# An encoder's dilated attention: the undilated head group over nearby keys with a softmax of its own, and the attention steps staggered anew

## The reference

```python
B_GROUPS = ((128, 1), (512, 4), (2048, 16))      # (window, dilation), 4 heads each
def dilated_attention(q, k, v, window, dilation):
    # to_sub gathers each residue class mod dilation by stride
    o, lse = banded_attention(to_sub(q), to_sub(k), to_sub(v), (window // 2) // dilation, None)
...
    qa, ka, va = ...                              # 8 query heads, 2 key heads, |i-j| <= 128, with sinks
    ya, _ = banded_attention(qa, ka, va, A_HALF_WINDOW, a_sink[l])
    for gi, (win, dil) in enumerate(B_GROUPS):
        o, lse = dilated_attention(qg, kg, vg, win, dil)
        outs.append(o); lses.append(lse)
    wg = jax.nn.softmax(jnp.stack(lses, axis=0), axis=0)
    yb = jnp.sum(wg[..., None] * jnp.stack(outs, axis=0), axis=0)
    merged = jax.nn.sigmoid(parts[-2]) * ya + jax.nn.sigmoid(parts[-1]) * yb
    x = x + jnp.einsum('bsd,de->bse', merged, w_out[l])
```

## Time and profile before

| | before |
| --- | --- |
| time, median of 3 runs | 1340.33 us (1340.04 to 1347.6) |
| profiled execution, its own time | 1341.68 us |
| span of the profiled execution | 1339.9 us |
| mean granted TensorE clock | 0.972 |
| PE busy | 1216.8 us (91%) |
| PEld (weight load, beside PE) | 798.0 us (60%) |
| DVE busy | 574.7 us (43%) |
| ACT busy | 410.5 us (31%) |
| POOL busy | 232.7 us (17%) |

### The profile page before, as it was taken

One profiled execution on the slowest core, in us unless ns is written; L12 is line 12 of the kernel. 1 busy time (PEld: TensorE's weight loads), 2 busy tenths in 40 slices (PEclk: granted clock), 3 DMA queues, 4 the chain that ended last, 5 costly groups with the idle time before them and its releaser, 6 DMA issues.

```text
span 1339.9 us, 17202 instructions
## 1 busy us (share of the span) xinstructions
PE 1216.8 (91%) x6364; PEld 798.0 (60%) x6364; DVE 574.7 (43%) x1359; ACT 410.5 (31%) x768; POOL 232.7 (17%) x179
## 2 busy tenths in 40 slices
PE   6999989999999999888599999899999989988981
PEld 5777767888876343332177777678887844433320
DVE  5567676333345222221455777743333442222115
ACT  5334346333342110000334443563332411110002
POOL 0314140122201111111012323302221011111100
PEclk9999999999999999899899999999999889999996
DMA  5432221553556999999823323126537379999995
GB/s 213 119 99 88 79 80 33 173 203 107 208 219 208 420 426 422 424 421 411 306 81 95 97 92 95 33 79 209 168 96 297 141 278 411 423 424 424 420 412 221
DMA packets 69566, 306.62 MB, mean 229 GB/s; under 512 B 11968, under 2 KB 12224, under 8 KB 59248
## 3 DMA queue, kind: packets, MB, share of 16 engines
q1 hardware_dynamic: 58624, 282.45, 56.0%
q0 software_dynamic: 10720, 22.37, 4.5%
q10 hardware_dynamic: 144, 0.77, 0.2%
HBM read 290.34 MB, written 23.07 MB: 234 GB/s over the span
## 4 chain that ended last, share of the span: by engine, by line
PE 64%; DMA 12%; SPq 8%; DVE 8%; ACT 4%; issue 2%; DVEq 2%; POOLq 0%; ACTq 0%
PE bank L508 13%; PE bank L510 13%; PE bank L509 13%; PE bank L792 10%; DMA gu<-in_gu_w 9%; SPq L368 5%; PE bank L808 5%; SPq L373 3%; DMA raw<-in_stream 2%; PE bank L648 2%; PE bank L787 1%; DVE prob L1295 1%; PE bank L618 1%; DVEq L1272 1%; PE bank L588 1%
## 5 line engine op out<-in xcount | busy, mean ns | idle before, releaser
L792 PE MATMUL bank<-gu,xgt 128*64 128x512 f32 x1024 | 237.8, 613 | 39.8 <-DMA gu<-in_gu_w 38.0
L508 PE MATMUL bank<-h_hi,w_hi 128*128 128x512 f32 x640 | 253.3, 396 | 8.1 <-DVE w_lo L1175 4.0
L510 PE MATMUL bank<-h_hi,w_lo 128*128 128x512 f32 x640 | 249.5, 390 | 0.0
L509 PE MATMUL bank<-h_lo,w_hi 128*128 128x512 f32 x640 | 249.1, 389 | 0.0
L792 PEld LDWEIGHTS bank<-gu,xgt 128*64 128x64 f32 x1024 | 74.8, 141 | 198.8 <-issue 150.8
L1175 DVE TENSOR_TENSOR w_lo<-raw,w_hi 128x1024 fp32r<-128x1024 f32 x102 | 124.4, 1220 | 145.8 <-ACT w_hi L920 144.5
L508 PEld LDWEIGHTS bank<-h_hi,w_hi 128*128 128x128 f32 x640 | 120.1, 188 | 34.8 <-issue 8.1
L510 PEld LDWEIGHTS bank<-h_hi,w_lo 128*128 128x128 f32 x640 | 120.1, 188 | 25.7
L509 PEld LDWEIGHTS bank<-h_lo,w_hi 128*128 128x128 f32 x640 | 120.3, 188 | 23.6
L920 ACT ACTIVATE w_hi<-raw 128x1024 fp32r<-128x1024 f32 x102 | 107.5, 1054 | 59.7 <-PE bank L510 56.2
L808 PE MATMUL bank<-dn,zt 128*64 128x512 f32 x512 | 117.2, 599 | 6.3 <-ACT zt L1134 2.8
(11 more groups left out here) (173 smaller groups left out, 1600.5 us busy)
## 6 DMA issues: line engine op xcount, KB each, us to landing
gu<-in_gu_w SPq DMA_DIRECT2D x18, 4096.0 KB, 31.6
raw<-in_stream SPq DMA_DIRECT2D x112, 512.0 KB, 3.6
dn<-in_dn_w SPq DMA_DIRECT2D x18, 2048.0 KB, 32.3
gu<-in_gu_w SPq DMA_DIRECT2D x32, 1024.0 KB, 14.9
dn<-in_dn_w SPq DMA_DIRECT2D x20, 1024.0 KB, 19.0
gu<-in_gu_w SPq DMA_DIRECT2D x32, 512.0 KB, 4.9
swp<-pj SPq DMA_DIRECT2D x136, 64.0 KB, 2.2
dn<-in_dn_w SPq DMA_DIRECT2D x16, 512.0 KB, 5.5
```

The source lines that it names most:

```text
L508: mm(dst, ah, bh, start=start, stop=False)
L509: mm(dst, ah, bl, start=False, stop=False)
L510: return mm(dst, al, bh, start=False, stop=stop)
L792: last = mm(bank[b][e * CAP:(e + 1) * CAP, :], xgt[:, x_s, k, e * CAP:(e + 1) * CAP], gu[w_s][:, e, k, :], start=k == 0, stop=k == KD - 1)
```

## The change

The undilated group keeps its queries and keys in natural order. A step's 128 queries then need 256 keys only, in two runs of 128 (`CHUNKS`), and the near and the two far groups get softmaxes of their own: `max_b` and `sum_b` hold minimum and sum of each, the near values go to bank 7 and the far ones to bank 3, and at the end the near weight is the sigmoid of the difference of the log-sums (`logs`, `lse`, `mix`, `near_weight`, `join`), which PE spreads over 64 rows by matmuls of a repeated column with the identity. Values come one step late in all steps, scores three ahead; the 16 tiles are spread over steps 0 to 11, 13, 14, 16 and 18 (`FILLED`); ACT copies the transposed probabilities before it does the exponentials. In the last block of tiles the values tiles come after queries and keys.

```diff
+BLOCK_C = BLOCK_B[3:] + BLOCK_B[:3]
+BLOCKS = [BLOCK_A, BLOCK_B, BLOCK_C]
...
+FILLED = (*range(12), 13, 14, 16, 18)
+NB = 2 * NSTEP_B
+CHUNKS = [(0, 1), (1, 2), (2, 3), (3, 0)]
+def score_bank(u, h):
+    if u < NSTEP_A:
+        return (2, 0, 1, 3)[2 * (u % 2) + h]
+    return (2 * (u - NSTEP_A) + h + 2) % 3
...
-    order += [("scores", 0), ("scores", 1)]
+    order += [("scores", 0), ("scores", 1), ("scores", 2)]
...
-    for u in range(NSTEP_A):
+    for u in range(STEPS):
         order.append(("transpose", u))
-        next_tile()
-        order.append(("scores", u + 2))
-        order.append(("values", u))
-    next_tile()
-    order.append(("scores", NSTEP_A + 2))
-    for u in range(NSTEP_A, STEPS):
-        order.append(("transpose", u))
-        if u > NSTEP_A:
+        if u in FILLED:
+            next_tile()
+        elif waiting:
+            order.append(("turn", waiting.pop(0)))
+        if u == STEPS - 5:
+            order.append(("split", NQ))
+        if u == STEPS - 4:
+            order.append(("split", NQ + 1))
+        if u == STEPS - 3:
+            order += [("gate", 0), ("lse", 0)]
+        if u == STEPS - 2:
+            order.append(("split", NQ + 2))
+        if u:
             order.append(("values", u - 1))
         if u + 3 < STEPS:
             order.append(("scores", u + 3))
-        if u == STEPS - 4:
-            order.append(("split", NQ))
-        if u == STEPS - 3:
-            order.append(("gate", 0))
-    order += [("values", STEPS - 1), ("gate", 1)]
+    order += [("mix", 0), ("mix", 1), ("join", 0), ("values", STEPS - 1), ("join", 1), ("gate", 1)]
...
-                        pe.wait_ge(ptd_ok, l * NSTEP_A + len(before))
+                        pe.wait_ge(pta_ok, l * STEPS + len(before))
+                        pe.wait_ge(ptd_ok, l * NSTEP_A + min(len(before), NSTEP_A))
...
+                        if u > NSTEP_A:
+                            pe.wait_ge(mh_ok, l * NB + u - NSTEP_A)
+                        c0, c1 = CHUNKS[r]
+                        for n in ([None] if c0 and c1 else [0, 1]):
+                            for h in range(2):
+                                rows = slice(h * DH, (h + 1) * DH)
+                                dst = bank[score_bank(u, h)]
+                                if n is None:
+                                    mm(dst[:, 0:MG], qk[rows, 0, cols], qk[rows, 1, c0 * P - 64:(c1 + 1) * P - 64], start=True, stop=True)
+                                else:
+                                    mm(dst[:, n * P:(n + 1) * P], qk[rows, 0, cols], chunk(qk[rows, 1, :], CHUNKS[r][n]), start=True, stop=True)
...
+                        parts_of = [(7, [(vb[:, 0, k, :], n * P) for n, k in enumerate(CHUNKS[t])]),
+                                    (3, [(vb[:, g, t, :], (g + 1) * P) for g in (1, 2)])]
+                    for b, terms in parts_of:
+                        for n, (v, c0) in enumerate(terms):
+                            for h in range(2):
+                                last = mm(bank[b][h * DH:(h + 1) * DH, cols], v[:, h * DH:(h + 1) * DH], pt[u % 2][:, h, c0:c0 + P],
+                                          start=n == 0, stop=n == len(terms) - 1)
...
+                def mix(p, l=l):
+                    if p == 0:
+                        pe.wait_ge(lse_ok, l + 1)
+                        pe.wait_ge(pj_act, (l + 1) * NQ)
+                        need(pe, mx_ok, (l + 1) * STEPS)
+                    dst = bank[6 if p == 0 else 2]
+                    for kind in range(2):
+                        for t in range(TT):
+                            for h in range(2):
+                                one = 4 * (p * NSTEP_B + t) + 2 * h + kind
+                                half = dst[h * DH:(h + 1) * DH, :]
+                                out = by_residue(half)[:, t, :, :] if kind else half[:, t * P:(t + 1) * P]
+                                last = mm(out, lse_b[:, one:one + 1].to_broadcast([P, DH]), ident, start=kind == 0 and t == 0,
+                                          stop=kind == 1 and t == TT - 1)
+                    last.then_inc(dm_ok, 1)
...
+                            for kind in range(2):
+                                p = prob[u % 3][:, h, kind * MG:(kind + 1) * MG]
+                                one = 4 * (u - NSTEP_A) + 2 * h + kind
+                                last = run(p, p, ACT.Exp, bias=max_b[:, one:one + 1], scale=-1.0, accum_out=sum_b[:, one:one + 1])
...
+                    last = run(pt[u % 2][:, 0, 0:width(u)], bank[4][:, 0:width(u)], ACT.Copy)
+                    if u >= NSTEP_A:
+                        last = run(pt[u % 2][:, 1, :], bank[5][:, :], ACT.Copy)
+                    last.then_inc(pta_ok, 1)
...
+                def logs(l=l):
+                    act.wait_ge(ex_ok, (l + 1) * STEPS)
+                    run(lse_b, sum_b, ACT.Ln).then_inc(ln_ok, 1)
+                    run(spare, ms[:, 0:1], ACT.Sigmoid)
+                def near_weight(p, l=l):
+                    act.wait_ge(dm_ok, l * 2 + p + 1)
+                    run(w_near[:, p, :], bank[6 if p == 0 else 2][:, :], ACT.Sigmoid).then_inc(wn_ok, 1)
+                def join(p, l=l):
+                    act.wait_ge(of_ok, l * 2 + p + 1)
+                    run(o_hi[:, 4 + p, :], o_near[:, p, :], ACT.Copy).then_inc(ohi_ok, 1)
...
+                        if i + 2 < STEPS:
+                            exps(i + 2)
...
+                    if u >= 3:
+                        dve.wait_ge(tr_ok, l * STEPS + u - 2)
...
+                            v.tensor_tensor_reduce(out=prob[u % 3][:, h, 0:MG], in0=src[:, 0:MG], in1=mask_b[:, (r + 1) // 2, :],
+                                                   scale=-SCALE, scalar=3.0e38, op0=ALU.add, op1=ALU.min, accum_out=max_b[:, one:one + 1])
+                            last = v.tensor_tensor_reduce(out=prob[u % 3][:, h, MG:MB], in0=src[:, MG:MB], in1=mask_b12[:, :],
+                                                          scale=-SCALE, scalar=3.0e38, op0=ALU.add, op1=ALU.min,
+                                                          accum_out=max_b[:, one + 1:one + 2])
+                            last.then_inc(mx_ok if h else mh_ok, 1)
...
+                def lse(l=l):
+                    dve.wait_ge(ln_ok, l + 1)
+                    logs, tops = (a.rearrange("p (n k) -> p n k", k=2) for a in (lse_b, max_b))
+                    tt(logs[:, :, 0], logs[:, :, 0], tops[:, :, 0], ALU.subtract)
+                    tt(logs[:, :, 1], tops[:, :, 1], logs[:, :, 1], ALU.subtract).then_inc(lse_ok, 1)
+                def join(p, l=l):
+                    dve.wait_ge(wn_ok, l * 2 + p + 1)
+                    o = o_near[:, p, :]
+                    v.drain()
+                    tt(o, o, w_near[:, p, :], ALU.mult)
+                    v.drain()
+                    tt(o, o, o_far[:, p, :], ALU.add).then_inc(of_ok, 1)
+                    dve.wait_ge(ohi_ok, l * 6 + 4 + p + 1)
+                    tt(o_lo[:, 4 + p, :], o, o_hi[:, 4 + p, :].bitcast(FP32), ALU.subtract).then_inc(olo_ok, 1)
```

More of the change, by code:

```diff
@@ L591, in scores @@
                                 rows = slice(h * DH, (h + 1) * DH)
[L592 removed]
+                                last = mm(bank[score_bank(u, h)][:, (g + 1) * P:(g + 2) * P], qk[rows, 2 * g, cols],
                                           qk[rows, 2 * g + 1, cols], start=True, stop=True)
@@ L646, in values @@
-                    for n, (v, c0) in enumerate(terms):
-                        for h in range(2):
-                            last = mm(bank[7][h * DH:(h + 1) * DH, cols], v(h), pt[u % 2][:, h, c0:c0 + P],
-                                      start=n == 0, stop=n == len(terms) - 1)
-                    last.then_inc(pv_ok, 1)
+                        parts_of = [(7, [(vb[:, 0, k, :], n * P) for n, k in enumerate(CHUNKS[t])]),
+                                    (3, [(vb[:, g, t, :], (g + 1) * P) for g in (1, 2)])]
@@ L1288, in normalise @@
                         v.reciprocal(den[:, two], den[:, two])
-                    else:
-                        n = MB
-                        v.reciprocal(den[:, two], rsum[:, two])
-                    v.drain()
-                    for h in range(2):
-                        p = prob[u % 3][:, h, 0:n]
-                        last = ts(p, p, den[:, 2 * s + h:2 * s + h + 1], None, ALU.mult)
+                        v.drain()
+                        for h in range(2):
+                            p = prob[u % 3][:, h, 0:n]
+                            last = ts(p, p, den[:, 2 * s + h:2 * s + h + 1], None, ALU.mult)
+                    else:
+                        u0 = 4 * (u - NSTEP_A)
+                        v.reciprocal(den_b[:, 4 * s:4 * s + 4], sum_b[:, u0:u0 + 4])
+                        v.drain()
+                        for h in range(2):
+                            for kind in range(2):
+                                p = prob[u % 3][:, h, kind * MG:(kind + 1) * MG]
```

(12 more changed lines are left out.)

182 lines of the change are left out of this document (81 added, 101 removed).

## The result

| | after | before, same chip |
| --- | --- | --- |
| time, median of 9 runs each | 1334.47 us (1329.83 to 1340.11) | 1342.83 us (1339.25 to 1347.6) |
| profiled execution, its own time | 1330.62 us | 1341.68 us |
| span | 1328.8 us | 1339.9 us |
| mean granted TensorE clock | 0.969 | 0.972 |
| PE busy | 1203.0 us | 1216.8 us |

The ratio of the times is 0.994 (95% interval 0.9916 to 0.9963): 8.4 us less, where 14.8 were forecast. The chance most in favour was faster by over 1%; what came is within 1%, and the median lies 0.5 us above the range.

The account below looks back on a forecast made before the run. PE was taken to bound attention. Per layer 11.6 us saved, less 3.9 for the mix and 9.1 of new waits, plus 8.8 of old losses, made 7.4; two layers 14.8, so 1325.5 us, range 1317 to 1334.

Parts of the forecast that it names:

- The walk: Attention's new order followed step by step through PE, ACT and DVE: PE's waits were to come to 9.1 us a layer.
- turns: Turns of values tiles in steps 15, 17 and 19 wait for copies out of bank 5: 1.4, 1.2 and 1.2 us.
- transposes 23: Last step's transposes wait 1.9 us for ACT's copy of step 22, behind the logarithm and two table loads.
- scores 2: Now among the first scores, in the bank of number 0, they wait 0.6 us for DVE's minimum.
- The join: Joining near and far halves at attention's end: ready near 32.5 us, hidden under gate 1 with half a microsecond to spare.
- (a): Undilated group over 256 keys, not 512: less PE work in scores, transposes and values, 11.6 us saved a layer.
- (b): Mixing the two softmaxes with 32 matmuls (64 records) adds 3.9 us of PE work a layer.
- the wait of step 12: In step 12, without a tile, PE waits 1.2 us for DVE's minimum, copy and normalisation before transposes 13.
- rival 1: A lower clock in the shortened steps: two falls a layer lose 3.1 us, giving 1331.7 us; chance 0.20.
- Single waits cost no clock: Argument against a slower kernel: single waits in the old trace, of 1.2 and 0.3 us, left matmul lengths unchanged.
- The reordering gives nothing: Spread tiles, late values, early scores and copies first: new waits 9.1 against 8.8 us of old losses, net minus 0.3.
- rival 2: The logarithm's table loads cost twice, so transposes 23 wait 2.6 us more: 1330.7 us; chance 0.05.

Follow-up runs that it names:

- e4: The kernel before, with PE kept at work by constant matmuls in its two long waits; the fillings overran: 1348.35 us, ratio 1.0023.
- e1: The changed kernel run again without any edit, for a second profile: 1333.07 us, ratio 0.9913 to the kernel before.
- e11: The changed kernel with one tile moved from step 13 to step 12: 1334.8 us, ratio 0.9934 to the kernel before.
- e8: The changed kernel with the tiles back in steps 0 to 15, one each: 1325.94 us, ratio 0.9872 to the kernel before.
- e3: The changed kernel with the turns behind the values in steps without a tile: 1335.22 us, ratio 0.9922 to the kernel before.
- e5: The changed kernel with the halves of the gates' weights made earlier, after the scores of steps 18 and 20: 1329.25 us, ratio 0.99 to the kernel before.
- e7: The changed kernel with PE kept at work in its six long waits by constant matmuls 256 columns wide: 1331.02 us, ratio 0.9906 to the kernel before.
- e10: The changed kernel with the mix cut to one matmul per pair and head, output wrong: 1330.77 us, ratio 0.9917 to the kernel before.
- e6: The changed kernel with turns behind the values, gate weight halves earlier, logarithm and first-branch halves later: 1326.77 us, ratio 0.9882 to the kernel before.
- e9: The changed kernel with tiles in steps 0 to 15, turns behind values, weight halves and logarithm moved: 1328.09 us, ratio 0.989 to the kernel before.
- e2: The changed kernel with PE kept at work by constant matmuls 512 columns wide, which overran the waits: 1342.71 us, ratio 0.9981 to the kernel before.

## Why the prediction failed

**The walk held.** The waits come to 9.36 us in layer 1, forecast 9.1: turns 1.41, 1.38, 1.38 (1.4, 1.2, 1.2), transposes 21 0.74 (0.9), transposes 23 1.58 (1.9), scores 2 0.59 (0.6), vt 0.3, scores 23 none (0.4). The join was hidden with 0.6 us (0.5). The clock's share of the old losses is shown by e4. The mechanism of the walk was right. Two terms of the sum were mis-sized, and a third was put at nothing.

**The step that failed most: the price of (a).** It was put at 11.6 and is smaller by some 1.2 us a layer: eight transposes took 1.02 for 0.93, sixteen values records 1.03 (204.16 to 205.19) for 0.97, eight times. The prediction had priced a short run of records as a part of a long one (the first 8 of 12 transposes, two thirds of the values). By the rows, four transposes fewer save 1.46 - 1.02 = 0.44 us, not 0.53, and a third of the values 1.46 - 1.03 = 0.43, not 0.49. (b), the mix, gave 0.4 back: 3.49 for 3.9.

**The second: the wait of step 12.** It was put at 1.2 and measured 1.94, 1.90, 2.21 and 1.32, on average 0.6 us a layer more. I costed DVE's work there as if POOL did nothing beside it, though before's own trace has it in the same step:

```profile
156.77 3.38 DVE L1295 TENSOR_SCALAR prob<-prob,small 128x256 f32<-128x256 f32 x2
157.95 2.05 POOL L1640 TENSOR_TENSOR qk_b<-rca,swp 128x512 f32<-128x512 f32 x1
```

It isn't only scalings that stretch: in e1 the `rca` of 0.68 us took 2.52 at 152.09, in e11 a w_lo of 1.21 took 3.08 at 157.78, each beside POOL's product into `qk_b`. And it explains a second wait, which the walk had at 0.6: in layer 1 scores 2 waited 0.59 us in four of the eleven profiled executions of the new order and 1.27 to 1.59 in the other seven. DVE's subtraction of two columns (L1338 in after) and POOL's product into `qk_a` start there within half a microsecond of each other. In after DVE is first (60.57, POOL 60.68) and takes 0.16; in e8 it is second:

```profile
60.69 1.16 DVE L1338 TENSOR_TENSOR small<-small,par 128x2 f32<-128x2 f32 x1
60.57 1.26 POOL L1716 TENSOR_TENSOR qk_a<-rca,swp 128x512 f32<-128x512 f32 x1
```

It ends with POOL's product (61.85 and 61.83). It is so in all eleven: first, 0.16 (after, e3, e5, e7); second, 0.84 to 1.16 (the others). No run took POOL's work away, so the cause is read from this agreement.

**The third, put at nothing: the clock, rival 1 in small.** "Single waits cost no clock" is not a rule: in layer 2 of the changed kernel and in both layers of e10 a fall of 1.5 to 1.6 us stood behind waits of step 12 of 1.90, 1.94 and 1.74; behind 1.94, 2.21 and 1.32 (after, e1) and 2.60 (e3, e5) there was none. Over the profiled executions that leave this wait as it is (after, e1, e3, e5, e6, e10) it is 3 layers in 12, 0.4 us a layer, not the 3.1 of the rival. The two falls of e3 stood behind other waits, 1.86 and 2.36.

Together, from 7.4: waits -0.5 (idle 9.36, 9.52, 10.32 and 9.06 in the four layers of after and e1, for 9.1), (a) -1.2, (b) +0.4, the clock -0.4, which makes 5.7. The four samples show 6.2; 0.5 us stay unaccounted for. Attention fell short by 2.3 us an execution.

**"The reordering gives nothing"** was right as a balance of the whole and hid a choice. e8 shows that with all else as changed the spread of the tiles costs 3.0 us a layer. But it isn't the spacing as such: once the turns, the weights' halves and the logarithm have been moved, spread (e6) and unspread (e9) attention take the same, 169.8 us on average. By the rows of e8 the spread costs what it exposes: two turns right behind transposes (2.8 us) and the wait of step 12 (1.9), less what the waits in steps 16 to 23 grew. If the reordering as a whole came out even, its gain was in its other parts; which of them, no run here tells.

**What stays open.** Of the 6.4 us between the forecast of 14.8 and the measured 8.4 (5.0 to 11.3 by the interval), the terms above explain 2.3; the other 4.1, the larger part, isn't in attention as its traces show it, and its cause stays open. A part may be chance: the two profiled executions differ by 11.1 us, and e1's ratio gives 11.7 (7.6 to 15.6). The rest of the span, from the first scores of layer 1 on and without the two attentions, was 918.9 and 923.9 us in the two executions of the old order (before, e4) and 919.8 and 923.0 in the two of the changed kernel: a spread of 3 to 5 us in either, with no side. In the nine others of the new order it was 921.1 to 926.0. The base too was low: the prediction stood on 1340.33 from three runs, and the kernel before ran at 1342.8 to 1344.2 in all later groups.

Yet chance alone is a poor account. In all eleven profiled kernels of the new order the median of the whole gained less on before than the two attentions (and the wait for o_lo, where it came) did on before's trace, by 0.8 to 5.7 us, 2.8 on average. Two readings are left. Something behind attention takes a part back; the first request for expert weights did move with the end of attention (0.12 us behind it in before and after), and between the attentions PE waited 18.2 us for these weights in before, 16.5 and 16.7 in after and e1, so they don't show it. Or before's one trace makes its attention too long: its layers have a fall of 1.57 and 1.62 us (863.77 - 857.73 for 4.42), and whether every execution of that kernel has them no run shows. More profiles of the kernel before would decide.

**The Trainium skill on table loads.** The two switches of the logarithm took 222.44 to 223.73 and 223.98 to 225.27: 1.29 us each, with ACT at work right ahead and behind. The Trainium skill, ScalarE: Activation LUTs, section "What ACT_TABLE_LOAD costs", adds a drain of about 1380 ns to each. The trace doesn't agree; the measurement decides, and rival 2 is out.

## What to carry to other kernels

Where the steps without cover work stood mattered by 3.0 us a layer while turns and weight halves stood where they did, and by nothing once these had been moved (e6 and e9). So look first at what stands right behind the transposes in such a step, and then at the spacing. Before a wait is costed, look in the old trace at what its releaser's engine does in that very step, and what its neighbour does beside it, not at the shortest row of the same form. A run of records has a part that a shorter run keeps, so a share of the long run's time is too low a price. When a wait is taken out, ask for what stands behind it in the releaser's queue: 2.4 for 2.9 us came back under another name in e3, 3.8 for 4.6 in e9. And a gain in idle time can go to the clock, as in e3.

## What the hardware showed that I had not expected

- A scaling of 128x256 on DVE is 0.3 us alone; two took 3.46 while POOL did products of 128x512 of 1.29 and 2.05 us. A subtraction of two columns took 0.16 when it started 0.03 to 0.13 us ahead of POOL's product, and until that product's end when it started 0.12 us or more behind it, in all eleven executions.
- The same wait of about 1.9 us is followed by a fall of the granted clock (0.62 over 4 us) in layer 2 and by none in layer 1 of the same execution.
- A float32 matmul of 512 columns took 0.86 us with 128x128 weights (e2). With half the weights' rows or columns and two side by side, two took 0.96 (scores) and four 1.72 (e10): half the price each.
